# Attention mixer of a two-block layer: projection units in another order, the halves of a rotation exchanged by transfers

## The reference, cut to what matters

```python
h = rms_norm_2(x, g_mix[l])
proj = h @ w_in[l]                                   # 256 x 1024 @ 1024 x 2304
qa, ka, va, qd, kd, vd = jnp.split(proj, splits, axis=-1)
qa = apply_rope(qa...); ka = apply_rope(ka...)       # 8 query heads, 2 key heads of 64
out_a = sliding_window_sink_attention(qa, ka, va, sinks[l])
qd = apply_rope(qd...); kd = apply_rope(kd...)       # 4 heads x 2 halves of 64
a = softmax(q1 k1) - lam * softmax(q2 k2)            # differential attention
od = rms_norm_2(a @ vd, g_diff) * (1 - lam_init)
x = x + concatenate([out_a, od]) @ w_out[l]
# apply_rope: x1, x2 = split(x, 2); [x1*c - x2*s, x2*c + x1*s]
```

## Time and profile before

| | us |
|---|---|
| median of three runs | 983.21 (981.7 to 983.92) |
| the profiled execution | 985.29 |
| its span, first to last instruction | 983.5 |
| mean granted clock of TensorE, share of full | 0.994 |
| TensorE busy | 943.8 (96%) |
| VectorE busy | 663.1 (67%) |
| ScalarE busy | 557.2 (57%) |
| GpSimd busy | 20.8 (2%) |

### The profile page before, as it was taken

One profiled execution on the slowest core, in us unless ns is written; L12 is line 12 of the kernel. 1 busy time (PEld: TensorE's weight loads), 2 busy tenths in 40 slices (PEclk: granted clock), 3 DMA queues, 4 the chain that ended last, 5 costly groups with the idle time before them and its releaser, 6 DMA issues. The chain is left out here.

```text
span 983.5 us, 17862 instructions
## 1 busy us (share of the span) xinstructions
PE 943.8 (96%) x6332; PEld 815.2 (83%) x6332; DVE 663.1 (67%) x1097; ACT 557.2 (57%) x1018; POOL 20.8 (2%) x47
## 2 busy tenths in 40 slices
PE   9999999989989999999999999987998999999997
PEld 8888888889988878888888888977777888888885
DVE  5776666677776467766667786798367366666665
ACT  7555555477445236555555676977566446454442
POOL 3002000000000001000000000000000000000000
PEclk9999999999999999999999999999999999999999
DMA  8777666455220246666666665642156236665652
GB/s 240 216 231 221 195 184 186 142 150 140 72 67 3 65 121 166 202 188 190 187 185 200 177 191 151 175 126 87 44 150 193 68 123 193 191 196 174 199 182 85
DMA packets 204241, 153.75 MB, mean 156 GB/s; under 512 B 5323, under 2 KB 189872, under 8 KB 204192
## 3 DMA queue, kind: packets, MB, share of 16 engines
q1 hardware_dynamic: 202896, 151.08, 51.5%
q0 software_dynamic: 1296, 2.01, 0.9%
HBM read 152.02 MB, written 1.05 MB: 156 GB/s over the span
## 5 line engine op out<-in xcount | busy, mean ns | idle before, releaser
L486 PE MATMUL ps<-XT,whi 128*128 128x512 f32 (+1 forms) x1728 | 519.5, 363 | 5.8 <-DVE XT L1787 5.0
L486 PE MATMUL ps<-XT,wlo 128*128 128x256 f32 x1440 | 403.8, 282 | 0.1
L1742 DVE TENSOR_TENSOR wlo<-raw,whi 128x1024 fp32r<-128x1024 f32 x277 | 332.9, 1222 | 98.0 <-ACT whi L1224 76.7
L486 PEld LDWEIGHTS ps<-XT,whi 128*128 128x128 f32 x1728 | 307.3, 190 | 62.7 <-issue 8.6
L1224 ACT ACTIVATE whi<-raw 128x1024 fp32r<-128x1024 f32 x277 | 288.8, 1054 | 46.5 <-PE ps L486 11.9
L486 PEld LDWEIGHTS ps<-XT,wlo 128*128 128x128 f32 x1440 | 272.8, 190 | 3.4 <-DVE wlo L1742 0.5
L486 PE MATMUL ps<-whi,H 128*128 128x512 f32 x608 | 177.7, 393 | 0.4 <-DVE H L2410 0.4
L486 PEld LDWEIGHTS ps<-whi,H 128*128 128x128 f32 x608 | 109.0, 188 | 23.3 <-DVE H L2410 0.7
L486 PE MATMUL ps<-wlo,H 128*128 128x512 f32 x304 | 95.7, 393 | 0.0
L486 PE MATMUL ps<-arena 64*64 64x64 f32 (+6 forms) x1512 | 88.1, 245 | 6.4 <-ACT arena L1421 1.7
L486 PEld LDWEIGHTS ps<-arena 64*64 64x64 f32 (+3 forms) x1512 | 80.4, 150 | 13.2 <-issue 2.5
(11 more groups left out here) (263 smaller groups left out, 720.2 us busy)
## 6 DMA issues: line engine op xcount, KB each, us to landing
raw<-in_ffn_w_gate SPq DMA_DIRECT2D x43, 512.0 KB, 4.6
raw<-in_ffn_w_up SPq DMA_DIRECT2D x43, 512.0 KB, 3.8
raw<-in_ffn_w_down SPq DMA_DIRECT2D x43, 512.0 KB, 4.6
raw<-in_w_in SPq DMA_DIRECT2D x36, 512.0 KB, 4.0
raw<-in_w_up SPq DMA_DIRECT2D x32, 512.0 KB, 4.0
raw<-in_w_down SPq DMA_DIRECT2D x32, 512.0 KB, 4.6
raw<-in_w_out SPq DMA_DIRECT2D x16, 512.0 KB, 3.4
raw<-in_w_ckv SPq DMA_DIRECT2D x16, 512.0 KB, 4.5
```

The lines of the kernel that those rows point to most:

```text
L486: return pe.matmul(o, st, mv, start=start, stop=stop, skip_group_check=True)
L1742: dve.tensor_tensor(wlo[:, n % RING, :], raw_of(n), whi[:, n % RING, :].bitcast(F32), sub).then_inc(lo_ready, 1)
```

## The change

It does five things, all within the attention mixer.

- The units come in another order: differential queries and keys in pairs (i = 0 to 7), the windowed key (8), the differential values (9 to 12), the windowed queries (13 to 16), the windowed values (17). Score tiles, transposes, maxima, exponents and reciprocals get places in this order from tables (`SCORES_AT`, `TURN_AT`, `MAX_AT`, `EXP_AT`, `INVERT_AT`).
- The partners of a rotation: ScalarE copies the unit's 128x256 out of PSUM to SBUF once (`QCP`) and then issues four transfers, SBUF to SBUF, of 32 partitions each, on its own queue. VectorE keeps only the product with the cosine. GpSimd multiplies the exchanged tile by the signed sine and adds (`rope_sin`, `rope_done`).
- After the units: the last two differential probability tiles' turn, the output products (second token half first), the last value unit's transposes, then score tiles 8 and 9, the normalised tiles' transposes, and score tiles 10 and 11. Before, all scores stood among the units.
- Banks: the differential outputs and their transposes in 2 and 3 (before 4 to 7), score tiles 8 to 11 in 4 to 7. VectorE takes `maxima(8)` ahead of the reciprocals of the differential norm, and the rest of the windowed tiles after it. The table of the square root is brought ahead of the squares.
- The first and the fourth output unit are issued in halves, with other work between.

The diff, with long or repeated parts left out:

```diff
@@ -273,6 +273,8 @@
         CVT = ar(21504, NT, D)
         CLOW = ar(23552, 2, T)
         SWP = CLOW
+        QCP = ar(24064, 2, T)
+        RSW = LWG[:, 0:T]
...
+        rope_arg, rope_tab, lam_arg, lam_exp, q_copy, q_sum, ksw_ready, rope_sin, rope_done = \
...
+        swp_in = [ctx.enter_context(nc.semaphore(f"swp_in{i}")) for i in range(2)]
...
-        VALUES = (13, 14, 15, 16, 17)
+        VALUES = (9, 10, 11, 12, 17)
...
         ORDER = [6, 7, 8, 9, 10, 11, 0, 2, 1, 3, 4, 5]
-        COLS2 = [6, 7, 8, 9, 10, 11, 12, 13, 0, 1, 2, 3, 4, 5, 14, 15, 16, 17]
+        COLS2 = [6, 10, 7, 11, 8, 12, 9, 13, 4, 14, 15, 16, 17, 0, 1, 2, 3, 5]
+        ROPED = [i for i, k in enumerate(COLS2) if k < 5 or 6 <= k < 14]
-        U_BANKS, TURN_BANKS = (4, 5, 6), (7, 7, 7, 3, 3, 4, 5, 4, 5)
+        U_BANKS, TURN_BANKS = (4, 5, 6), (7, 7, 7, 4, 5, 6, 7, 4, 5)
+        SC_BANKS = (0, 1, 2, 0, 1, 2, 0, 1, 4, 5, 6, 7)
+        SCORES_AT, TURN_AT = {5: (0,), 9: (1,), 10: (2,), 16: (3,)}, {10: 0, 14: 1}
+        MAX_AT = {5: 0, 6: 1, 9: 2, 10: 3, 11: 4, 12: 5, 16: 6, 17: 7}
+        EXP_AT = {6: 0, 7: 1, 10: 2, 11: 3, 12: 4, 13: 5, 17: 6}
+        INVERT_AT = {7: 0, 8: 1, 11: 2, 12: 3, 13: 4, 14: 5}
...
                 def scores(p):
 
-                    for k in (2 * p, 2 * p + 1):
-                        if k >= 3:
-                            pe.wait_ge(sc_sum, k - 2)
+                    if p in (1, 2):
+                        pe.wait_ge(sc_sum, 2 * p - 1)
+                    elif p == 3:
+                        pe.wait_ge(sc_sum, 5)
+                    elif p == 4:
+                        pe.wait_ge(q_sum, N_WIN2)
+                    elif p == 5:
+                        pe.wait_ge(vt_ev, 5)
...
@@ -1007,12 +1021,10 @@
                             pe.wait_ge(pt_ev, k)
                     else:
                         pe.wait_ge(sc_exp, 6 + k - 3 + 1)
-                        if k == 3:
-                            pe.wait_ge(vt_ev, 5)
-                        elif k in (5, 6):
-                            pe.wait_ge(od_norm, k - 4)
+                        if k < 7:
+                            pe.wait_ge(sc_sum, 6 + k)
                         else:
-                            pe.wait_ge(pt_ev, k if k == 4 else k - 1)
+                            pe.wait_ge(pt_ev, k - 3)
                     for i, (j, m, kb) in enumerate(BLOCKS[g]):
                         nk = (JOBS[j][1] + 1) * P
...
-                n_vt = 0
-                for i in range(N_WIN2 + 1):
-                    if i < N_WIN2:
-                        if i >= 3:
-                            pe.wait_ge(q_sum, i - 2)
-                        a_unit_summed(B_WIN2 + i, PS[U_BANKS[i % 3]], None if i else "mix2")
...
-                    if i == 7:
-                        pe.wait_ge(rope_done, 6)
-                        scores(0)
-                    if i == 9:
-                        pe.wait_ge(rope_done, 8)
-                        scores(1)
-                    if i == 11:
-                        scores(2)
-                    if i == 13:
-                        pe.wait_ge(rope_done, 13)
-                        pe.wait_ge(ksw_ready, 1)
-                        scores(3)
-                    if i in (15, 17):
-                        scores(i // 2 - 3)
-                    if i in (12, 14, 16):
-                        turn(i // 2 - 6)
-
...
+                def turn_value(i, n, bank):
+
+                    pe.wait_ge(q_sum, i + 1)
...
+                def diff_out(n):
+
                     for h in range(4):
-                        o = PS[4 + n][:, h * P:(h + 1) * P]
+                        o = PS[2 + n][:, h * P:(h + 1) * P]
...
-                turn(3)
-                turn(4)
+
+                for i in range(N_WIN2):
+                    if i >= 3:
+                        pe.wait_ge(q_sum, i - 2)
+                    a_unit_summed(B_WIN2 + i, PS[U_BANKS[i % 3]], None if i else "mix2")
+                    if i - 1 in VALUES:
+                        n = VALUES.index(i - 1)
+                        if n:
+                            pe.wait_ge(vt_ev, n)
+                        turn_value(i - 1, n, 3)
+                    if i in SCORES_AT:
+                        pe.wait_ge(rope_done, {5: 4, 9: 8, 10: 8, 16: 11}[i])
+                        if i == 16:
+                            pe.wait_ge(ksw_ready, 1)
+                        scores(SCORES_AT[i][0])
+                    if i in TURN_AT:
+                        turn(TURN_AT[i])
+
...
+                turn(2)
+                pe.wait_ge(vt_ev, 4)
+                diff_out(1)
+                pe.wait_ge(sc_sum, 6)
+                pe.wait_ge(pt_ev, 3)
+                diff_out(0)
+                turn_value(N_WIN2 - 1, 4, 7)
+                pe.wait_ge(rope_done, 13)
+                scores(4)
                 for b in range(2):
                     for n in range(NT):
                         pe.wait_ge(od_norm, n + 1)
                         for h in (2 * b, 2 * b + 1):
-                            last = pe.transpose(PS[6 + b][:, (h % 2) * T + n * P:(h % 2) * T + (n + 1) * P],
+                            last = pe.transpose(PS[2 + b][:, (h % 2) * T + n * P:(h % 2) * T + (n + 1) * P],
                                                 ODN[:, n, h * P:(h + 1) * P], ident)
                     last.then_inc(odt_mm, 1)
+                scores(5)
+                pe.wait_ge(sc_sum, 8)
+                for n in range(NT):
+                    pe.wait_ge(yt_ready, N_MIXED + (4 if n else 1))
+                    b_half(B_WOUT2, 0, XT[:, OUT2_ROWS[0], :], n, start=True)
+                turn(3)
+                turn(4)
+                output(1)
                 turn(5)
                 turn(6)
-                pe.wait_ge(sc_sum, 12)
-                pe.wait_ge(pt_ev, 5)
-                output(0, start=True)
+                output(2)
                 turn(7)
                 turn(8)
-                output(1)
-                output(2)
-                pe.wait_ge(pt_ev, 9)
-                pe.wait_ge(yt_ready, N_MIXED + 4)
                 for n in (1, 0):
+                    pe.wait_ge(pt_ev, 7 if n else 9)
...
-                output(3)
+                b_half(B_WOUT2 + 3, 0, XT[:, OUT2_ROWS[3], :], 0)
+                pe.wait_ge(os_norm, 3)
+                pe.wait_ge(pt_ev, 9)
                 for b in range(2):
                     for c in (2 * b, 2 * b + 1):
                         for n in range(NT):
-                            pe.wait_ge(os_norm, 3)
                             last = pe.transpose(PS[4 + b][:, (c % 2) * T + n * P:(c % 2) * T + (n + 1) * P],
                                                 OSN[:, n, c * P:(c + 1) * P], ident)
                     last.then_inc(odt_mm, 1)
+                b_half(B_WOUT2 + 3, 0, XT[:, OUT2_ROWS[3], :], 1)
                 for i in range(4, KC):
...
-                n_vt = n_rope = 0
-                for i in range(N_WIN2 + 1):
-                    if i < N_WIN2:
-                        split_to(B_WIN2 + i + LEAD + 1)
-                        if i not in VALUES:
-                            act.wait_ge(unit_used, B_WIN2 + i + 1)
-                            if n_rope >= 2:
-                                act.wait_ge(rope_done, n_rope - 1)
-                            for a, b in ((0, 1), (1, 0), (2, 3), (3, 2)):
-                                ins = act.activation(SWP[QUADRANTS[a], n_rope % 2, :],
-                                                     PS[U_BANKS[i % 3]][QUADRANTS[b], 0:T], ACT.Copy)
-                            ins.then_inc(q_swap, 1)
-                            n_rope += 1
+                def value_turned(i, n, bank):
...
+                    act.wait_ge(vt_mm, n + 1)
+                    for tt in range(NT):
+                        ins = act.activation(VT2[:, tt, at * P:(at + 1) * P], PS[bank][:, tt * P:(tt + 1) * P], ACT.Copy,
+                                             scale=RR[:, tt:tt + 1])
+                    ins.then_inc(vt_ev, 1)
...
+                    act.wait_ge(pv_mm, 2 - n)
+                    for h in range(4):
+                        ins = act.activation(ODJ[:, (4 * n + h) * P:(4 * n + h + 1) * P], PS[2 + n][:, h * P:(h + 1) * P],
+                                             ACT.Square, accum_out=ODS[:, 4 * n + h:4 * n + h + 1])
+                    ins.then_inc(od_ss, 1)
+
+                for i in range(N_WIN2):
+                    split_to(B_WIN2 + i + LEAD + 1)
+                    if i in ROPED:
+                        r = ROPED.index(i)
+                        act.wait_ge(unit_used, B_WIN2 + i + 1)
+                        if r >= 2:
+                            act.wait_ge(swp_in[r % 2], 64 * (r // 2))
+                        act.activation(QCP[:, r % 2, :], PS[U_BANKS[i % 3]][:, 0:T], ACT.Copy).then_inc(q_copy, 1)
+                        act.wait_ge(q_copy, r + 1)
+                        if r >= 2:
+                            act.wait_ge(rope_sin, r - 1)
```

(77 more changed lines are left out.)

60 lines of the change are left out of this document (17 added, 43 removed).

## The result

The changed kernel takes 996.1 us, median (994.89 to 997.51), against 983.57 us of the kernel before on the same chip: ratio 1.0117, 95% interval 1.0097 to 1.0137, so 11.5 us slower by the ratio and 12.5 by the two medians. The forecast was 978.2 us, with 987.5 as the upper end of its range. The profiled execution took 995.7 us, with a span of 993.9 and a mean granted clock of 0.985 (before: 985.3, 983.5 and 0.994).

The account below looks back on a forecast made before the run. TensorE, busy 96%, bounds the kernel, with VectorE setting the pace from 640 to 684 us. Losses of 14.1 us become 8.0 us of waits and up to 3.2 of clock; gain 5.0: 983.2 - 5.0 = 978.2 us, range 973 to 987.5.

Parts of the forecast that it names:

- What bounded the kernel before: TensorE busy 96% of the span; from 640 to 684 us VectorE, busy 41.05 of 44 us, sets the pace.
- 14.1 us of waits and clock: From 610.2 to 722.8 us TensorE loses 10.9 us in waits and 3.2 us in lowered clock.
- The price of an issue: On ScalarE each transfer issued costs 0.37 us, ends 0.1 and 0.55, making a rotated unit 2.9 us.
- The landing: A rotation's transfer lands in 2.2 us, kept between 1.9 and 3.0, within a path of 5.57 us.
- the lag: ScalarE's delay behind a unit's end: 1.6, 1.1 and 2.9 us at ropes 3, 7 and 10; hidden under 0.2.
- GpSimd: 0.9 was taken: Each of GpSimd's two operations in a rotation takes 0.9 us, with 0.6 and 1.6 as ends.
- The rival in which VectorE holds GpSimd back: VectorE's splits stretch GpSimd's operations to 1.6 us; waits 12.4 us, gain 0.2, 983.0 us; chance 0.20.
- Three waits for rotations: TensorE waits 1.4, 1.0 and 2.3 us for rotated tiles behind units 5, 9 and 16.
- The tail: After the output products TensorE waits 2.6 and 0.4 us for normalised tiles, in place of 2.98, behind VectorE's tile 8.
- The clock: Two slow stretches of TensorE stay, behind the waits of 2.3 and 2.6 us, costing up to 3.2 us.
- The slower rival: ScalarE becomes the bound at 0.55 us an issue, 3.6 us a rotated unit against 2.88: 986.1 us; chance 0.20.
- the middle of 2.9 and 6.7: Whole kernel's gain lies between 2.9 us and 6.7 us; 5.0 us was taken as the middle.

Follow-up runs that it names:

- the shorter fill: Changed kernel with 27, 19 and 22 extra products of ones by ones on TensorE ahead of its three waits for rotations: 993.49 us, ratio 1.0091.
- the variant with copies: Changed kernel with four 32-partition ScalarE copies out of PSUM in place of the four transfers; order and GpSimd's part stay: 977.84 us, ratio 0.9926.

## Why the prediction was wrong, point by point

**What bounded the kernel before: right.** The new order is a gain (3 to 6 us by its interval), and VectorE's relief seems to be one. The prediction's 14.1 us of waits and clock were there to be had, and the new order with GpSimd, at the old price of an exchange, took 7 of them.

**The price of an issue: the step that failed.** "I take 0.37, the row that is nearest in size and kind, and keep 0.1 and 0.55." Measured 0.51 for the first and 0.61 for each further one, above the upper end. With what stands between them that is 3.90 us of ScalarE in a rotated unit where 2.9 was forecast: 1.0 us for each, and the first nine units are all rotated. Nearest in size was the wrong nearness: all rows read DRAM, and these read SBUF. The rows of 0.33 us were also issued with time between (some 6 us), and these stand four in a row. The runs with SyncE and with a DRAM source show both differences. GpSimd's 546 ns was nearer only by luck: it is another engine's issue, and it reads DRAM too.

Rows that would have warned were in the trace of the kernel before, at its start, where SyncE issues without time between. The row of 0.37 us is the second of that run; later ones are not so cheap, and "0.33 to 0.37 whatever the size" does not hold for them:

```profile
1.20 0.37 SPq L412 DMA_DIRECT2D arena<-in_ffn_norm  x1
...
2.96 0.58 SPq L402 DMA_DIRECT2D raw<-in_ffn_w_up  x1
3.58 3.59 SPq L402 DMA_DIRECT2D raw<-in_ffn_w_gate  x1
```

GpSimd issues transfers there as well. What makes an issue so long there, no run here shows.

**Issues on a queue are not free of the other queues.** The Trainium skill (Perfetto Trace Analysis, "DMA Instruction — HWDGE (DVE, Sync)") says that the window shown for an issue takes in the wait for the descriptor generator, which is locked for exclusive use, and lasts until all descriptors are made and the queue is free. The trace agrees in part: ScalarE's two issues take 1.41 us beside SyncE's, against 1.15 without, but SyncE's two take 1.14 in the same time, so the exclusive part can't be the whole window. The same skill (DMA: Bandwidth & Descriptors, "Issuing engines are not separate DMA queues") calls the time that issuing from several engines saves "usually small relative to the DMA itself". Not here: four issues take 2.44 us, about as long as one of these transfers takes to land (median 2.4), and issuing from two engines saved 17.5 us of the kernel.

**The landing: too short.** 2.2 was taken, 3.0 was the end. The median is 2.4, but GpSimd waits for the last of four, and that one landed 3.69 us after its issue began. Copy and wait 0.39, three issues 1.83, landing and wait 3.76, GpSimd 1.55: 7.53 in place of 5.57. By itself this is 1.5 us in each of three waits; it is not what makes the lag grow.

**GpSimd: 0.9 was taken, 0.72 to 0.88 came** for 24 of the 26 operations, and 1.59 and 1.80 for two. They took 21.1 us in all, 0.81 each. The prediction's estimate of 0.56 us for an addition is too low here: 0.73. The rival in which VectorE holds GpSimd back is wrong in its size, though the mechanism is there (below).

**Three waits for rotations:** 1.4, 1.0 and 2.3 were forecast, 6.12, 4.35 and 5.04 came. The places were right. The first can be taken apart: unit 3 ends at about 621.8 us and its copy begins at 627.21, a lag of 5.4 us where 1.6 was forecast. 5.4 + 7.53, less the 6.85 us until TensorE is through unit 5 (628.66), makes 6.1. So the lag gave 3.8 us more than forecast and the path 2.0, and 1.1 came off for TensorE's later end. The first grew the most because nothing gives ScalarE time to catch up before it; each wait lets it catch up, which is why they don't add.

**The tail: right,** in its mechanism too. 2.6 + 0.4 was forecast and 2.73 + 0.16 came; the output products end at 696.36 us, the root of the squares is done 1.9 us later, and VectorE's maximum of tile 8 is the last, as said.

**The clock: the second term that was mis-sized.** Two slow stretches of 3.2 us in all were forecast. There are four, and by their granted clock they cost (1-0.58) x 6.8 + (1-0.54) x 7.1 + (1-0.65) x 6.8 + (1-0.67) x 5.1 = 10.2 us behind the waits. Waits 19.2 and clock 10.2, less the 10.9 and 3.2 of before, make 15.3 us; the stretch grew by 13.05. The clock's part of this sum is too large. Over the two stretches TensorE's idle time grew by 8.1 us (11.15 to 19.24) and its busy time by 5.0 (101.40 to 106.37), where the granted clock would have it grow by 7.0. What makes up the other 2 us is open.

**The slower rival was the right one:** ScalarE the bound, deciding from about 0.5 us an issue. Its time, 986.1, was 10 us short for two reasons. It was worked out at 0.55 and gave waits of 15.5 us in place of 19.2; and it put the clock at 1.5 us, less than the forecast's own, though its waits were longer than those that had cost 3.2. A bound of a cost that decides, carried at the wrong clock, made the range end at 987.5.

**Two sums of the prediction are off,** by too little to matter: the middle of 2.9 and 6.7 is 4.8 and not 5.0, and in the rival on GpSimd 3.2 + 2.4 + 3.7 with the tail of 3.3 us make 12.6 and not 12.4.

## What to carry to other kernels

Before a copy on a compute engine is traded for transfers that the same engine issues, count what the issues hold of its queue: here 0.51 us for the first and 0.61 for each further one, against 0.38 us for the copy of a quarter that it replaced. The busy share doesn't show it, the queue's own rows do. If the transfers are wanted, a second issuing queue took the loss away here, and two larger ones in place of four took most of it; neither was faster than the copies. Look for the price of an issue where issues stand as they will stand in the change: four in a row, with the same source. And every wait that this adds on TensorE is to be costed with the slow stretch behind it: 15.5 us of waits brought 8.5 us of lost clock by the granted clock, of which 6 us net came back in the stretch with the shorter fill.

## What the runs showed of the hardware that was not expected

**GpSimd and VectorE hold each other off for whole instructions.** In the changed kernel and, below, in the variant with copies (start us, us):

```profile
623.32 0.74 POOL L2526 TENSOR_TENSOR LWG<-arena 128x256 f32<-128x256 f32 x1 [2.80 <-DMA arena<-arena]
624.14 1.59 POOL L2528 TENSOR_TENSOR arena<-arena,LWG 128x256 f32<-128x256 f32 x1
...
623.43 1.71 DVE L1772 TENSOR_TENSOR wlo<-raw,whi 128x1024 fp32r<-128x1024 f32 x1 [4.54 <-ACT whi L1240]
```

```profile
626.61 1.60 POOL L2526 TENSOR_TENSOR arena<-arena,LWG 128x256 f32<-128x256 f32 x1
...
626.32 1.30 DVE L1770 TENSOR_TENSOR wlo<-raw,whi 128x1024 fp32r<-128x1024 f32 x1 [0.66 <-ACT whi L1240]
```

GpSimd's product began at 623.32, the split 0.11 us later: the split took 1.71 us instead of 1.23, 0.5 us longer, and 0.6 us of GpSimd's 0.74 was left when it began. GpSimd's sum then began under the split and took 1.59: it ended 0.6 us after the split had. In the other kernel the split was first, and GpSimd's 0.74 us became 1.60, again ending 0.6 us behind it. By the rule of the Trainium skill (SBUF — State Buffer, "Who interferes with whom"), cited ahead of the result, whichever starts first holds the other off; both cases agree. It costs nothing in these two places, since the sums are ready long before TensorE asks; in the variant with two transfers a sum of 1.80 us stood right ahead of a wait.

**The slow stretch began within the long waits and was as long behind each of them.** The same columns as in the windows above, changed kernel, one stretch at the lower of the two levels, what lies on its two sides, and the one after the shorter wait:

```profile
633.20:633.60 0.40, 0.00 (x0) 0.00 (x0) 0.00 (x0) 0.00 (x0) 0.40 (x1) 1.00 0.36 82
633.60:640.50 6.90, 5.72 (x25) 4.90 (x26) 4.17 (x5) 2.39 (x3) 2.51 (x4) 0.51 0.63 182
640.50:642.00 1.50, 1.50 (x15) 1.50 (x14) 0.00 (x0) 0.38 (x1) 1.04 (x2) 1.00 0.26 74
701.90:705.40 3.50, 3.50 (x20) 2.99 (x21) 3.01 (x7) 2.18 (x9) 0.00 (x0) 0.51 0.00 0
```

TensorE ended its work at 628.66 us; the clock fell at 633.6, 1.2 us before the wait of 6.12 was over, and rose at 640.5. Behind the waits of 4.35 and 5.04 us the slow stretch was 6.9 us too (from 654.1 and 684.8). Behind the 2.73 us of the tail it was 3.5 us and began only 1.5 us after work had been taken up again. With 6.19 us of products on ones in place of the first wait the clock did not fall.

**What a queue issued before can make its next issue dearer:** a load of 512 KB takes SyncE 0.37 us by itself and 0.59 right behind four small transfers from SBUF to SBUF.
